# Hyena filters of a two-block network: spectra from 128-row products between the panels, other orders at the routing and behind the experts

## What is computed

```python
def first_block(x, ...):              # two layers
    ...                               # gated recurrence, dense SwiGLU, recurrence again
    x = x + moe_swiglu(h, router_w, w1, w3, w2)   # 8 experts, each row goes to 2
    return rms_norm(x, final_norm)

def hyena_filters(L, ...):
    h = sin(freq * (... z @ w1 ...))              # three small layers, 64 wide
    h = (h @ w3).reshape(L, 2, 2, D) * decay      # 64 -> 4096: direction, order, channel
    fwd, bwd = h[:, 0], h[:, 1]
    k = concatenate([fwd, zeros, bwd[1:][::-1]])  # 512 long
    return k / sum(abs(k))

def hyena_mixer(xn, w_in, ...):       # layers 0 and 3 of the second block
    p = xn @ w_in + b_in              # 1024 -> 3072
    p = conv_b + 3-tap convolution of p along the rows
    x1, x2, v = split(p)
    kf = rfft(hyena_filters(...))
    z = v
    for o, gate in enumerate((x1, x2)):
        z = gate * (long_conv(z, kf[:, o]) + fbias[o] * z)
    return z @ w_out + b_out
```

## Time and profile before

| | us |
|---|---|
| median of the three runs | 3016.56 |
| lowest, highest | 3014.93, 3017.8 |
| the profiled execution | 3014.79 |
| its span | 3013.0 |
| PE busy | 2937.0 (97%) |
| DVE busy | 2041.7 (68%) |
| ACT busy | 1635.5 (54%) |
| POOL busy | 305.0 (10%) |
| mean granted PE clock | 0.986 |

### The profile page before, as it was taken

One profiled execution on the slowest core, in us unless ns is written; L12 is line 12 of the kernel. 1 busy time (PEld: TensorE's weight loads), 2 busy tenths in 40 slices (PEclk: granted clock), 3 DMA queues, 4 the chain that ended last, 5 costly groups with the idle time before them and its releaser, 6 DMA issues.

```text
span 3013.0 us, 46709 instructions
## 1 busy us (share of the span) xinstructions
PE 2937.0 (97%) x20212; PEld 2692.5 (89%) x20212; DVE 2041.7 (68%) x1816; ACT 1635.5 (54%) x1619; POOL 305.0 (10%) x245
## 2 busy tenths in 40 slices
PE   8999999999989999999999899999899999999999
PEld 8999999999978888888788496999799999786999
DVE  6787665688668888888788565554655465665653
ACT  6456534545557767767677462545654454353442
POOL 1130210123010000000000202110011010112110
PEclk9999999999999999999999899999899999999999
DMA  7445555544559989989999050557155555431453
GB/s 237 148 144 165 171 178 187 182 140 153 166 192 374 348 341 353 376 336 349 338 376 364 25 168 15 182 175 243 45 182 175 189 182 176 146 112 57 142 181 126
DMA packets 359411, 613.14 MB, mean 204 GB/s; under 512 B 11455, under 2 KB 323733, under 8 KB 324384
## 3 DMA queue, kind: packets, MB, share of 16 engines
q1 hardware_dynamic: 355936, 597.99, 57.0%
q10 hardware_dynamic: 2784, 11.97, 1.2%
q0 software_dynamic: 480, 0.12, 0.0%
HBM read 608.99 MB, written 1.05 MB: 202 GB/s over the span
## 4 chain that ended last, share of the span: by engine, by line
PE 91%; DVE 4%; ACT 3%; issue 1%; DMA 1%; SPq 0%; POOLq 0%; POOL 0%; ACTq 0%; DVEq 0%
PE ps L329 18%; PE ps L331 18%; PE ps L330 18%; PE ps L1263 5%; PE ps L1265 5%; PE ps L1264 5%; PE ps L1244 3%; PE ps L1242 3%; PE ps L1243 3%; PE ps L1772 2%; PE ps L689 2%; PE ps L1787 2%; DVE wlo L273 2%; PE ps L1742 2%; ACT whi L262 1%; PE ps L1728 1%
## 5 line engine op out<-in xcount | busy, mean ns | idle before, releaser
L273 DVE TENSOR_TENSOR wlo<-raw,whi 128x2048 fp32r<-128x2048 f32 (+2 forms) x574 | 1317.2, 2300 | 596.6 <-ACT whi L262 592.3
L262 ACT ACTIVATE whi<-raw 128x2048 fp32r<-128x2048 f32 (+2 forms) x574 | 1083.7, 1891 | 267.0 <-PE ps L331 136.0
L329 PE MATMUL ps<-HX,whi 128*128 128x256 f32 x1808 | 517.7, 286 | 16.3 <-DVE wlo L273 11.5
L330 PE MATMUL ps<-HX,whi 128*128 128x256 f32 x1808 | 513.9, 284 | 0.0
L331 PE MATMUL ps<-HX,wlo 128*128 128x256 f32 x1808 | 513.8, 284 | 0.0
L329 PE MATMUL ps<-HXB,whi 128*128 128x256 f32 x1760 | 500.9, 285 | 6.7 <-DVE HXB L448 6.7
L330 PE MATMUL ps<-HXB,whi 128*128 128x256 f32 x1760 | 498.0, 283 | 0.0
L331 PE MATMUL ps<-HXB,wlo 128*128 128x256 f32 x1760 | 498.0, 283 | 0.0
L329 PEld LDWEIGHTS ps<-HX,whi 128*128 128x128 f32 x1808 | 349.2, 193 | 19.8 <-ACT HX L524 10.4
L330 PEld LDWEIGHTS ps<-HX,whi 128*128 128x128 f32 x1808 | 349.6, 193 | 0.3 <-issue 0.2
L331 PEld LDWEIGHTS ps<-HX,wlo 128*128 128x128 f32 x1808 | 349.3, 193 | 0.0
(11 more groups left out here) (331 smaller groups left out, 4343.3 us busy)
## 6 DMA issues: line engine op xcount, KB each, us to landing
raw<-in_c_experts SPq DMA_DIRECT2D x264, 1024.0 KB, 4.9
raw<-in_w_in SPq DMA_DIRECT2D x71, 1024.0 KB, 5.0
raw<-in_ff_w_gate SPq DMA_DIRECT2D x44, 1024.0 KB, 5.3
raw<-in_ff_w_up SPq DMA_DIRECT2D x44, 1024.0 KB, 5.3
raw<-in_ff_w_down SPq DMA_DIRECT2D x32, 1024.0 KB, 5.2
raw<-in_dense_w SPq DMA_DIRECT2D x30, 1024.0 KB, 5.3
raw<-in_hy_w_in SPq DMA_DIRECT2D x24, 1024.0 KB, 5.2
raw<-in_ff_w_down SPq DMA_DIRECT2D x16, 768.0 KB, 4.7
```

Of the source, the lines that this page charges most:

```text
L262: e.activation(m.whi[:, i % NSPLIT, 0:n], m.raw[:, i % NRAW, 0:n], ACT.Copy).then_inc(*k.up("act", "hi", i))
L273: e.tensor_tensor(m.wlo[:, i % NRAW, 0:n], m.raw[:, i % NRAW, 0:n], hi, ALU.subtract).then_inc(*k.up("dve", "lo", i))
L329: e.matmul(o, wh, xh, start=first and t == k0, stop=False)
L330: e.matmul(o, wh, xl, start=False, stop=False)
```

## The change

The features of the backward direction are put into the other 64 partitions, so that a product has 128 rows and gives forward plus backward (even) or forward minus backward (odd) at once: `filter_rows` now has `plus` (both halves as they are) and `minus` (one half negated). One half is moved across by a DMA of ACT's queue (`act_features_across`); `pool_backward` does the rest. Stationary operands are taken with a step of two columns, so that even and odd places come apart; the transform matrix is reordered so that 128 frequencies are enough, and each pair of results is added and subtracted by DVE for the lower and upper half of the spectrum. `PIECES` are the four pieces of a spectrum, `FILTER_TURNS` says behind which panel each stands.

```diff
 def pe_filters(e, k, m, s, f, o_):
...
-    for d, x in ((0, hs), (1, hb)):
-        if d:
-            e.wait_ge(*k.at("backward", s))
+    e.wait_ge(*k.at("backward", s))
+    for d in range(2):
...
-                cc = d * 2048 + o_ * 1024 + c * 512
-                e.matmul(o[:, :], x[:, j * 128:j * 128 + 128], fw3[:, cc:cc + 512], start=True, stop=True).then_inc(
+                cc = o_ * 1024 + c * 512
+                e.matmul(o[:, :], filter_rows(m, f)[d][:, j:L:2], w[:, cc:cc + 512], start=True, stop=True).then_inc(
+def pe_spectrum(e, k, m, s, o_, n):
+    part, c = PIECES[n]
...
+    for j in range(2):
+        o = pe_take(e, k, m, "spec", s, o_, part, c, j)
+        e.matmul(o[:, :], dft[:, part, j, 0:128], src[:, j * 1024 + c * 512:j * 1024 + c * 512 + 512],
+                 start=True, stop=True).then_inc(*k.up("mm", "spec", s, o_, part, c, j))
+def pe_l1(e, k, m, s, o_):
+    o = pe_take(e, k, m, "l1", s, o_)
+    e.wait_ge(*k.at("abs", s, o_))
...
+FILTER_TURNS = {0: ("spec", 0, 3), 2: ("l1", 0), 3: ("spec", 1, 0), 4: ("spec", 1, 1), 5: ("spec", 1, 2), 6: ("spec", 1, 3), 9: ("l1", 1)}
 def pe_hyena(e, k, m, s, last):
-    pe_spectra(e, k, m, s, last)
-    pe_gemm(e, k, m, s, "in", m.HX, range(12), fresh=("hx", last))
+    for n in range(3):
+        pe_spectrum(e, k, m, s, 0, n)
+    for j in range(12):
+        pe_gemm(e, k, m, s, "in", m.HX, [j], fresh=None if j else ("hx", last))
+        turn = FILTER_TURNS.get(j, ("",))
+        if turn[0] == "spec":
+            pe_spectrum(e, k, m, s, turn[1], turn[2])
+        elif turn[0] == "l1":
+            pe_l1(e, k, m, s, turn[1])
 def act_hyena(...)
...
     for j in range(12):
         act_panel(e, k, m, panels)
+        turn = FILTER_TURNS.get(j - 1, ("",))
+        if turn[0] == "spec":
+            act_spectrum(e, k, m, s, turn[1], turn[2])
+            if turn[2] == 3:
+                act_absolute(e, k, m, s, turn[1])
         e.wait_ge(*k.at("g", s, "in", j))
...
+            if c >= PADS:
+                e.wait_ge(*k.at("cv", s, c - PADS))
+def dve_spectrum_parts(e, k, m, s, o_, n):
...
+    e.tensor_tensor(lower, o, upper, ALU.add).then_inc(*k.up("dve"))
+    e.wait_ge(*k.own("dve"))
+    if part:
+        e.tensor_tensor(upper, upper, o, ALU.subtract)...
+def dve_absolute(e, k, m, s, o_):
+    x = m.buf(EVEN[o_])
+    e.wait_ge(*k.at("absolute", s, o_))
+    e.tensor_tensor(x, x, m.buf(ODD[o_]), ALU.max).then_inc(*k.up("dve"))
     e.wait_ge(*k.own("dve"))
+    e.tensor_tensor(x[:, 0:1024], x[:, 0:1024], x[:, 1024:2048], ALU.add).then_inc(*k.up("dve", "abs", s, o_))
 def dve_hyena(...)
...
         dve_panel(e, k, m, panels)
+        turn = FILTER_TURNS.get(j - 1, ("",))
+        if turn[0] == "spec":
+            dve_spectrum_parts(e, k, m, s, turn[1], turn[2])
+        elif turn[0] == "l1":
+            dve_factors_l1(e, k, m, s, turn[1])
+        turn = FILTER_TURNS.get(j - 2, ("",))
+        if turn[0] == "spec" and turn[2] == 3:
+            dve_absolute(e, k, m, s, turn[1])
```

Behind the experts:

```diff
-def crowded(e, k, m, path, *args):
+def crowded_flag(e, k, m):
-    for name in ("mm", "act", "dve", "pool"):
-        e.wait_ge(*k.at("places filled", name))
-    with e.If(e.value_load(m.over[0:1, 0:1], min_val=0, max_val=1) > 0):
+    e.wait_ge(*k.at("over"))
+    return e.value_load(m.over[0:1, 0:1], min_val=0, max_val=1)
+def crowded(e, k, m, flag, path, *args):
+    with e.If(flag > 0):
+        for name in ("mm", "act", "dve", "pool"):
+            e.wait_ge(*k.at("places filled", name))
 def act_moe(...)
         if x == 6:
-            act_hyena_loads(e, k, m, a, 0, ("ga", s, 3, 7), ("gt free", s, 2))
+            e.wait_ge(*k.at("ga", s, 3, 7))
+            act_features_across(e, k, m, 0)
...
+        if x == 7:
+            e.wait_ge(*k.at("gt free", s, 2))
+            act_hyena_loads(e, k, m, a, 0)
 def pe_program(...)
-    pe_filters(e, k, m, "hy0", 0, 0)
     pe_hold(e, k, m, "sum", "moe")
     pe_sums(e, k, m, "moe", 0, 8)
     k.release("sum", "moe")
-    pe_filters(e, k, m, "hy0", 0, 1)
+    pe_filters(e, k, m, "hy0", 0, 0)
     pe_hold(e, k, m, "sum", "final")
     pe_sums(e, k, m, "final", 0, 8)
     k.release("sum", "final")
+    pe_filters(e, k, m, "hy0", 0, 1)
```

More of the change, by code:

```diff
@@ L1207, in pe_moe @@
     e.wait_ge(*k.at("msk", s))
[L1208 to L1212, removed]
+    e.matmul(o[:, 0:16], upper, ms, start=True, stop=False)
+    e.matmul(o[:, 8:16], m.ones[:, :], ms[:, 0:8], start=False, stop=True).then_inc(*k.up("mm", "rank", s))
+    o = pe_take(e, k, m, "count", s)
+    e.matmul(o[:, 0:16], m.ones[:, :], ms, start=True, stop=True).then_inc(*k.up("mm", "count", s))
+    flag = crowded_flag(e, k, m)
     pe_gather(e, k, m, v, s, 0)
@@ L1234, in pe_moe @@
             wh, wl = weights(m, n, 2, 1024)
[L1235 to L1239, removed]
+            if j % 2 == 0:
+                e.wait_ge(*k.at("hid", s, x, j // 2))
+            for c in range(2):
+                for kk in range(2):
+                    t = 2 * j + kk
                     cs = slice(c * 512, c * 512 + 512)
@@ L1486, in dve_moe @@
     dve_scatter(e, k, m, s, 3)
+    return flag
 def dve_turn_hidden(e, k, m, s, x, j):
@@ L1535, in pool_rows @@
 def pool_rows(e, k, m, s, last):
+    e.wait_ge(*k.at("gated", s, 0))
     e.wait_ge(*k.at("ht", s, 1, 1))
@@ L1672, in crowded @@
         e.wait_ge(*k.at("o end", "o_dve"))
[L1679 removed]
+EVEN, ODD, KR, KI = (7, 10), (9, 11), (1, 7), (2, 8)
 DECAY = (4, 8)
+PADS = 6
+PIECES = [(part, c) for part in range(2) for c in range(2)]
+FILTER_TURNS = {0: ("spec", 0, 3), 2: ("l1", 0), 3: ("spec", 1, 0), 4: ("spec", 1, 1), 5: ("spec", 1, 2), 6: ("spec", 1, 3), 9: ("l1", 1)}
 def pads(m):
[L1684 to L1688 removed]
+    rows = m.buf(0)[:, 0:PADS * (L + 2)].rearrange("p (t n) -> p t n", t=PADS)
+    return [rows[:, c % PADS, :] for c in range(24)]
 def dft_view(m):
@@ L1695, in filter_rows, with filter_halves, act_hyena_loads, act_features_across @@
 def filter_rows(m, f):
-    half = slice(64 * f, 64 * f + 64)
-    return m.hsb[half, :], m.small[half, :], m.HXP[half, :]
+    if f:
+        return m.hsb[:, :], m.small[:, :], m.buf(6)
+    return m.HXP[:, BUF:BUF + L], m.HXP[:, BUF + L:BUF + 2 * L], m.HXP[:, 0:BUF]
+def filter_halves(f):
+    return slice(64 * f, 64 * f + 64), slice(64 - 64 * f, 128 - 64 * f)
 def scale_columns(m, o_):
     return m.lbt[:, 36 + 8 * o_:44 + 8 * o_]
-def act_hyena_loads(e, k, m, a, f, *free):
-    for event in free:
-        e.wait_ge(*k.at(*event))
-    e.dma_start(filter_rows(m, f)[2], a["hy_f_w3_2"][f]).then_inc(*k.land("hy_in"))
+def act_hyena_loads(e, k, m, a, f):
+    w = filter_rows(m, f)[2]
+    for d, half in enumerate(filter_halves(f)):
+        e.dma_start(w[half, :], a["hy_f_w3_2"][f][:, d * BUF:d * BUF + BUF]).then_inc(*k.land("hy_in"))
     e.dma_start(m.buf(DECAY[f]).rearrange("p (j n) -> p j n", j=2), a["c_decay"]).then_inc(*k.land("hy_in", "hy_in", f))
+def act_features_across(e, k, m, f):
+    own, other = filter_halves(f)
+    e.dma_start(filter_rows(m, f)[0][other, :], m.hsb[own, :]).then_inc(*k.land("across_in", "across", f))
 def act_dft_load(e, k, m, a, s):
@@ L2471, in sp_program @@
     sp_constants(e, k, m, a)
-    sp_panels(e, k, m, panels, NRAW, ahead)
-    crowded(e, k, m, sp_crowded, a)
+    sp_panels(e, k, m, panels, NRAW, routed)
+    flag = crowded_flag(e, k, m)
+    sp_panels(e, k, m, panels, routed, ahead)
+    crowded(e, k, m, flag, sp_crowded, a)
     sp_panels(e, k, m, panels, ahead, len(panels))
@@ L2563, in dve_program @@
     dve_hgrn(e, k, m, panels, "hgrn1", "ffn0", 1, None)
-    dve_moe(e, k, m, panels, "moe", "hgrn1")
+    flag = dve_moe(e, k, m, panels, "moe", "hgrn1")
     for c in range(T8):
```

256 lines of the change are left out of this document (135 added, 121 removed).

## The result

The changed kernel takes 2976.11 us (median of 4 runs, 2973.89 to 2977.15), the kernel before, on the same chip, 3015.74 (4 runs, 3011.67 to 3017.8). The ratio is 0.9868, with a 95% interval of 0.9856 to 0.9881: 39.6 us less, forecast 39.6 less (2977 against 3016.6). That the two agree to the tenth is chance: the sum of the terms was 39.8 for the profiled execution, and the spans of the two profiled executions differ by 37.7. The profiled execution took 2977.15 us, with a span of 2975.3 and a mean granted PE clock of 0.988.

What follows compares the result with a forecast made beforehand. PE was taken as the bound, busy 2937.0 of 3013.0 us. First layer 19.3, second 11.2, expert 6 6.3 and routing 3.0 summed to 39.8 us less: 2975.0 for the profiled execution, forecast 2977, range 2958 to 2993.

Steps and rivals of the forecast that it cites:

- Behind the experts: From the last expert product to the first hyena panel: 40.8 us against 79.5, so 38.7 less.
- rival D: Hyena panels: the clock stays down behind the l1 wait, nine panels per layer at half clock, 3076 us; chance 0.02.
- The l1 wait: Before the first l1 group of each layer: PE waits 4.5 us for DVE's addition, then loses 2.5 to the clock.
- Rival A: First l1 group: no wait, both layers keep 7.0 us, total 2963; chance 0.2.
- Between the panels: Hyena panels, both layers: 12.4 us of PE work come back, with wait and clock loss 19.4 per layer.
- The step in the slices: Stationary slices taking every second column: priced at nothing, with 4.2 us per layer as the other end.
- Expert 6: Two hyena loads move to expert 7's end: panel wait 3.8 and half-clock loss 2.5 go, gain 6.3 us.
- The 4.2 us behind the experts: Part of PE's 6.08 us idle behind the last scatter, read as instruction fetch behind its block: claimed to stay.
- The copy: Behind the last expert: PE's 1.18 us wait for the copy of the last expert output goes.
- The routing: Before the gather: it starts at 859.5 instead of 862.7, gain 3.2 us, taken as 3.0.
- Rival B: Gather and behind experts: the flag costs PE its whole 5.4 us pause wherever read, total 2983; chance 0.12.
- Rival C: Between the panels: every piece holds PE, waits of some 3 us, total 3013, no change; chance 0.04.

Runs made afterwards that it cites:

- the four kernels without the l1 wait: Changed kernel with l1 group one panel later (2958.68 us); with DVE's maximum ahead of taps (2958.37); that plus flag behind gather (2956.6); that plus filter loads in four (2955.16).

## Why the prediction was right, step by step

**Behind the experts** was the largest term. Counted as in the forecast, from the last expert product, the stretch went from 79.5 to 40.2 us: 39.3 less, 38.7 forecast. 7.0 of it is the half clock of the filters. The forecast took the recovery behind the experts from expert 6 and gave the filters full clock; why they had been slow it left open. The runs settle it: 64 rows. In rival D the Trainium skill, "TensorE: Matmul & The Clock Gate", section "What's actually happening", stood with activity lifting the throttle; the record of 14.02 us at 0.50 shows PE fully busy and not lifted, so for products of 64 rows behind a pause the rule does not hold as it was read there.

**The l1 wait**, counted from the two queues, came out at 4.4 us where 4.5 were forecast. Its place, its releaser and its absence at the second group were right. Mis-sized was the clock behind it: 2.5 per layer in the term, 4.0 and 3.4 measured. Rival A has fallen: ACT's absolute values did end 8.1 us behind panel 0. Rival D has fallen: the clock is back 8 us after the wait, not after panels.

**Between the panels** 20.6 and 20.1 us came back per layer, with the clock's 1.5 and 0.9 over the 19.4 of the term. The other 1.2 and 1.0 us lie behind the first turn of z, where the same stretch differs by 5 us between kernels with equal code there. The table's 21.8 and 21.1 hold both.

**The step in the slices** was priced at nothing, with 4.2 us per layer as the other end. The records of the turns give some 0.3. The Trainium skill, "SBUF — State Buffer", section "Door 1: The DMA port swizzle", was read as a step of two without loss; the trace doesn't agree for the stationary loads of the turns, which went from 141 to 209 ns. As they run beside products, little of it reaches the time.

**Ahead of the second layer** 31.8 less, forecast 30.6: filters, sums and spectra all ran a little under their terms (6.86 for 7.1, 4.75 for 5.2).

**Expert 6** was 6.3 in the term. In the experts it was 5.2 to 5.7, but as an edit it is worth 3.0 to 3.7, because the moved loads lengthen PE's pause behind the experts.

**The 4.2 us behind the experts** were right by luck. The forecast took 1.9 off the 6.08 for addition and flag, and left 4.2 to the fetch. With no loads in flight the pause is 2.35, so addition and flag had cost 3.7, or 3.2 if the kernel before is taken with its sums first as well (5.50); the loads then put 1.9 back. Two errors of nearly the same size met. That the pause belongs to PE's block is what the kernel without the block shows. That it grows beside loads fits the Trainium skill, "Runtime: NRT & Kernel Launch", section "Instruction fetch mechanics", by which the target of a taken branch comes by DMA; the trace agrees in that much, with 2.35 and 4.25 us.

**The copy** was 1.18 and is 0.80: 0.4 gained, not 1.2.

**The routing** gained 2.9 of 3.0, in parts that differ: the flag stood at 859.0, 0.8 later than counted, and its load cost 1.0 us instead of 1.2. Rival B has fallen: its 5.4 us are a pause of the place behind the experts, not of a load. Rival C has fallen too: none of the five pieces between panels held PE.

## What to carry to other kernels

A wait on the bound engine can cost more than itself: the l1 wait of 4.4 us was followed by another 3.4 to 4.0 of clock, a pause of 2.35 behind the experts by 1.8, one of 1.5 by nothing. So a consumer is worth placing by counting its producers' queues, behind the last of them; that count was right to 0.1 us, and the l1 group one panel later, or DVE's maximum one panel sooner, would have been worth 17 us more. An edit that moves transfers is to be priced at the place where they arrive as well as where they leave. And after a pause the first products should be ones that bring the clock back, in this kernel those of 128 rows.

## What was not expected of the hardware

- Eight filter products behind a pause of 5.1 us took 8.7 us with 128 rows and 14.0 with 64; once at full clock, 64 rows stayed there (7.1 us).
- Waits of equal length cost different amounts of clock. Behind the pause of 4.0 to 4.3 us at the scatter the same sums took 5.38, 6.25 and 6.60 us in three kernels (3.6 at full clock). And ahead of the turn of z PE waits 2.6 to 2.7 us in all kernels; the eight transposes behind it took 1.1 us in the kernel before, 2.0 in the changed one, with and without the step, and 1.2 to 1.3 in the first layer of the four kernels without the l1 wait. In the kernel before, the products behind them run at half clock in the second layer and at full clock in the first:

```profile
2733.00:2736.00 3.00, 3.00 (x4) 1.04 (x4) 0.00 (x0) 3.00 (x8) 0.00 (x0) 0.51 0.00 0
...
1808.00:1811.00 3.00, 3.00 (x9) 1.33 (x8) 0.32 (x1) 3.00 (x8) 0.00 (x0) 1.00 0.00 0
```

- Executions with the same code up to there reach the gather between 859.7 and 862.5 us, and the attention's granted clock differs between profiles of equal code. So for 2 to 5 us only stretches of the timeline can be compared, and only short ones.
- PE's pause at the skipped block was 2.35 us without transfers in flight, and 3.9 to 4.3 with three loads in flight.
